# Prompt's attention between the k tiles of the gate panels, in a one-core decoder layer

## The reference

```python
h = rmsnorm(x); z = h @ w_in                       # q, k, v, u, s, m and three gates
o_da = differential attention (8 heads, T5 bias)   # prompt causal; samples over 512 paged keys + 8 new
o_sg = gelu(u) * (causal 128x128 mixing of rmsnorm(gelu(s)) + b)
o_mx = cross attention, 4 heads, 256 memory tokens # prompt: its own memory; samples: caches
gates = sigmoid(zg)
merged = g0 * (o_da @ wb0) + g1 * (o_sg @ wb1) + g2 * (o_mx @ wb2)
x = x + merged @ w_out
x = x + (silu(a) * b) @ w_down,  a, b = rmsnorm(x) @ w_up
y = rmsnorm(x)
```

## Time and profile before

| | us |
|---|---|
| median of 3 runs | 1431.42 (1426.54 to 1432.24) |
| the profiled execution, its own time | 1428.93 |
| its span, first to last instruction | 1427.2 |
| PE busy | 1322.6 (93%) |
| DVE busy | 674.5 (47%) |
| ACT busy | 553.8 (39%) |
| mean granted clock of TensorE | 0.98 |

### The profile page before, as it was taken

One profiled execution on the slowest core, in us unless ns is written; L12 is line 12 of the kernel. 1 busy time (PEld: TensorE's weight loads), 2 busy tenths in 40 slices (PEclk: granted clock), 3 DMA queues, 4 the chain that ended last, 5 costly groups with the idle time before them and its releaser, 6 DMA issues.

```text
span 1427.2 us, 26160 instructions
## 1 busy us (share of the span) xinstructions
PE 1322.6 (93%) x9982; PEld 1240.9 (87%) x9982; DVE 674.5 (47%) x1212; ACT 553.8 (39%) x1028; POOL 59.4 (4%) x106
## 2 busy tenths in 40 slices
PE   5789999999777799999998699999899999999995
PEld 4789999999545689889997369999899999999995
DVE  5452232224785122223333233337788888883333
ACT  5342321223586232323333254335555555562221
POOL 1010000000011001001000000000000000000000
PEclk9999999999999899999999999999899999999998
DMA  5355222624000977653452902222232222312221
GB/s 195 120 165 192 80 81 74 200 96 140 30 23 8 294 239 245 203 181 114 166 176 83 401 10 74 83 79 77 77 113 88 88 88 93 111 49 94 94 89 66
DMA packets 79768, 174.16 MB, mean 122 GB/s; under 512 B 5613, under 2 KB 40685, under 8 KB 78678
## 3 DMA queue, kind: packets, MB, share of 16 engines
q1 hardware_dynamic: 77942, 166.18, 34.8%
q0 software_dynamic: 1760, 7.08, 1.4%
HBM read 163.78 MB, written 11.82 MB: 123 GB/s over the span
## 4 chain that ended last, share of the span: by engine, by line
PE 55%; issue 30%; DVE 6%; ACT 3%; DMA 3%; POOL 1%; SPq 1%; DVEq 0%; POOLq 0%; ACTq 0%
PE acc L1837 46%; DMA km_pg<-mem_k 2%; DVE w_lo L1128 1%; PE ps L2074 1%; PE ps L2051 1%; ACT w_hi L666 1%; DVE logit_p L1346 1%; PE acc L2213 1%; DMA w_raw<-w_stream 1%; ACT p_junk L834 1%; ACT logit_p L818 1%; DMA b_sel<-bias_select 1%; DVE a_p L1369 1%; PE ps L1861 1%; PE ps L1954 0%
## 5 line engine op out<-in xcount | busy, mean ns | idle before, releaser
L1128 DVE TENSOR_TENSOR w_lo<-w_raw,w_hi 128x1024 fp32r<-128x1024 f32 x144 | 176.7, 1228 | 436.0 <-ACT w_hi L666 435.1
L1837 PE MATMUL acc<-h_hi,w_hi 128*128 128x288 f32 x1152 | 253.5, 302 | 1.8 <-issue 0.8
L1837 PE MATMUL acc<-h_hi,w_lo 128*128 128x288 f32 x1152 | 248.4, 297 | 0.0
L1837 PE MATMUL acc<-h_lo,w_hi 128*128 128x288 f32 x1152 | 248.4, 297 | 0.0
L666 ACT ACTIVATE w_hi<-w_raw 128x1024 fp32r<-128x1024 f32 x144 | 151.5, 1054 | 207.4 <-PE acc L1837 106.1
L1837 PEld LDWEIGHTS acc<-h_hi,w_hi 128*128 128x128 f32 x1152 | 184.6, 189 | 8.8 <-issue 6.3
L1837 PEld LDWEIGHTS acc<-h_lo,w_hi 128*128 128x128 f32 x1152 | 185.5, 189 | 0.0
L1837 PEld LDWEIGHTS acc<-h_hi,w_lo 128*128 128x128 f32 x1152 | 185.4, 189 | 0.0
L2267 PE MATMUL acc<-xs_hi,w_hi 128*128 128x288 f32 x352 | 105.7, 300 | 5.2 <-DVE w_lo L1551 4.2
L2267 PE MATMUL acc<-xs_hi,w_lo 128*128 128x288 f32 x352 | 106.0, 301 | 0.0
L2267 PE MATMUL acc<-xs_lo,w_hi 128*128 128x288 f32 x352 | 106.0, 301 | 0.0
(11 more groups left out here) (317 smaller groups left out, 2401.7 us busy)
## 6 DMA issues: line engine op xcount, KB each, us to landing
w_raw<-w_stream SPq DMA_DIRECT2D x166, 512.0 KB, 3.5
v_pg<-cache_v SPq DMA_DIRECT2D x32, 512.0 KB, 5.6
w_raw_b<-w_stream SPq DMA_DIRECT2D x22, 512.0 KB, 4.2
k_even<-cache_k SPq DMA_DIRECT2D x16, 512.0 KB, 6.1
k_odd<-cache_k SPq DMA_DIRECT2D x16, 512.0 KB, 6.2
km_pg<-mem_k SPq DMA_DIRECT2D x8, 1024.0 KB, 6.6
vm_pg<-mem_v SPq DMA_DIRECT2D x8, 1024.0 KB, 7.8
x_sb<-xT SPq DMA_DIRECT2D x8, 576.0 KB, 9.5
```

Source lines behind the costliest of these rows:

```text
L1128: nc.vector.tensor_tensor(w_lo[:, u, :], w_raw[:, u, :], w_hi[:, u, :].bitcast(F32), ALU.subtract)\
L1837: last = nc.tensor.matmul(acc[a][:, c, 0:n], w[:, u, k * P:(k + 1) * P], x[:, k0 + k, c * n:(c + 1) * n], start=start and k == 0 and t == ...
```

## The change

Eight gate panels of da_branch become a stage `da_gate` ahead of sg_branch, and prompt's attention runs inside them: after k tile k of panel c PE calls `p_step(8c + k)`. At odd steps it does turn_probs(n), values(n-1), score(n+2), n = (q-3)/2. Scores now use banks 4 and 5 alone, transposes bank 6, outputs bank 7. DVE's and ACT's order within attention is as before; ACT copies each head's output out of its bank first, and applies the gate's function after the fourth tile of a head, DVE splits the next weights after the first tile of the next head. The last steps of attention fall into the first two sg panels. Gates are stored to DRAM (`gate_d`) and loaded again for `da_proj`, eight projection panels of o_da in a row. The sigmoid becomes tanh(x/2); the 1.0 is added in the product and the 0.5 applied to `merged`. Samples begin at the half panels in S_UNIT, and SP's orders in the zone are sorted by the half panel at which they are due. The cut diff:

```diff
-STAGES = (... ("u", 8), ("sg_branch", 16), ("zm", 8), ("da_branch", 16), ("mx_branch", 16), ...)
+STAGES = (... ("u", 8), ("da_gate", 8), ("sg_branch", 16), ("zm", 8), ("da_proj", 8), ("mx_branch", 16), ...)
+S_UNIT = (2, 7, 13, 19, 24, 30, 36, 41)
 # SP
+            for c in range(KT):
+                load_w(FIRST["da_gate"] + 2 + c, c % 2)
+                if c:
+                    store_gate(c - 1)
+                if c + 2 < HEADS:
+                    sp.wait_ge(p_logit, QT * (c + 1))
+                    sp.dma_start(bias_p[c % 2], bias_pd[c + 2]).then_inc(p_bias[c % 2], 16)
+            store_gate(KT - 1)
+            for c in range(2):
+                load_w(FIRST["sg_branch"] + 2 + c, c)
+            sp.wait_ge(p_pv, TILES_P)
+            sp.wait_ge(v_zero, 1)
             value_pages(0)
+            sp.wait_ge(p_oss, HEADS)
             key_pages(1)
+            orders = [(2 * c - 1, "w", c) for c in range(2, 24)]
+            orders += [(S_UNIT[b] - 6 if b > 2 else S_UNIT[0], "k", b) for b in range(2, NB)]
+            orders += [(S_UNIT[b] - 3, "v", b) for b in range(1, NB)]
...
+            def load_gate(n):
+                if n >= 2:
+                    sp.wait_ge(acc_free[n % 2], FIRST["da_proj"] // 2 + n // 2)
+                sp.dma_start(g_slot[n % 2][:, :], gate_d[n]).then_inc(gate_loaded[n % 2], 16)
+            sp.wait_ge(gate_stored, 16 * KT)
+            sp.wait_ge(s_oout, NB)
+            load_gate(0)
+            load_gate(1)
             sp.wait_ge(o_lo_done, 2 * KT)
             for e in range(2):
+                load_w(FIRST["da_proj"] + 2 + 2 * e, 0)
+                load_gate(2 + 2 * e)
+                load_w(FIRST["da_proj"] + 3 + 2 * e, 1)
+                load_gate(3 + 2 * e)
                 mem_keys(e, e)
                 mem_values(e, e)
+            load_w(FIRST["da_proj"] + 6, 0)
+            load_gate(6)
+            load_w(FIRST["da_proj"] + 7, 1)
+            load_gate(7)
...          # kmT, vm_nat
+            stream(FIRST["da_proj"] + 8, FIRST["mx_branch"] + 2)
 # ACT, after o_split(qT, o_da[0])
-            branch("da_branch")
+            for n in range(KT):
+                p = FIRST["da_proj"] + n
+                act.wait_ge(mm_done, p + 1)
+                split_hi(p + 2, n % 2)
 # DVE
+            p_logits(0)
+            for n in range(TILES_P):
+                if n + 1 < TILES_P:
+                    p_logits(n + 1)
+                p_combine(n)
+                if n % QT == 2 and n > QT:
+                    p_norm(n // QT - 1)
+                if n % QT == 0 and n:
+                    split_lo(FIRST["da_gate"] + n // QT + 1, (n // QT - 1) % 2)
...
-            branch("da_branch")
+            for n in range(KT):
+                p, u = FIRST["da_proj"] + n, n % 2
+                split_lo(p + 2, u)
+                dve.wait_ge(mm_done, p + 1)
+                dve.wait_ge(gate_loaded[u], 16 * (n // 2) + 16)
+                wait(dve, merged_done, n)
+                nc.vector.scalar_tensor_tensor(halves(scaled[:, 0, :]), halves(g_slot[u][:, :]), 1.0, acc_t(u),
+                                               ALU.add, ALU.mult).then_inc(acc_free[u], 1)
 # PE
+            def p_step(q):
+                n = (q - 3) // 2
+                if q == 1:
+                    p_score(1)
+                if q % 2 and 0 <= n < TILES_P:
+                    p_turn_probs(n)
+                if q % 2 and 0 < n <= TILES_P:
+                    p_values(n - 1)
+                if q % 2 and 0 <= n < TILES_P - 2:
+                    p_score(n + 2)
+                if q % 8 == 0 and 0 <= q // 8 - 2 < HEADS:
+                    p_turn_out(q // 8 - 2)
+            p_score(0)
+            for c in range(KT):
+                slot_free("da_gate", c // 2, c % 2)
+                panel(FIRST["da_gate"] + c, c % 2, h_hi, h_lo, behind=lambda k: p_step(8 * c + k))
...
-            branch("da_branch", o_da, 2 * KT)
+            for n in range(KT):
+                slot_free("da_proj", n // 2, n % 2)
+                panel(FIRST["da_proj"] + n, n % 2, *o_da, tile_ready=da_tile if n == 0 else None)
```

More of the change, by code:

```diff
@@ L863, in _, with p_exps @@
-            pairs(act, p_body)
+            def p_exps(n):
+                m, e, i = n % 2, n // QT % 2, TILE_ORDER[n % QT]
+                w = (i + 1) * P
+                act.wait_ge(p_neg, n + 1)
+                wait(act, p_rc, n // QT - 1)
+                for c in range(2):
+                    last = nc.scalar.activation(logit_p[:, m, c, 0:w], logit_p[:, m, c, 0:w], ACT.Exp,
+                                                bias=col(P_NEG + 2 * m + c),
+                                                accum_out=col(P_SUM + m if c else P_S0 + 4 * e + i))
+                last.then_inc(p_exp, 1)
@@ new lines, in p_squares @@
+            def p_squares(h):
+                e = h % 2
+                act.wait_ge(p_copied, h + 1)
+                act.wait_ge(p_rc, h + 1)
+                wait(act, p_ost, 3 * (h - 1))
+                for i in range(QT):
+                    last = nc.scalar.activation(p_junk[:, i * DV:(i + 1) * DV], o_p[:, e, i * DV:(i + 1) * DV], ACT.Square,
+                                                scale=col(P_RC0 + 4 * e + i), accum_out=col(P_SS + 4 * e + i))
+                last.then_inc(p_oss, 1)
@@ L865, in s_exp_probs @@
+            p_copy(HEADS - 1)
+            p_squares(HEADS - 1)
             def s_exp_probs(b):
@@ L1395, in s_logits @@
+            split_lo(FIRST["da_gate"] + HEADS + 1, 1)
             def s_logits(b):
@@ L2038, in _, with p_score @@
-            for hp in range(HEADS // 2):
-                p_body(hp, hp == HEADS // 2 - 1)
+            def p_score(n):
+                h, i = n // QT, TILE_ORDER[n % QT]
+                w = (i + 1) * P
+                wait(pe, p_logit, n)
+                for c in range(2):
+                    rows = slice(c * DK, (c + 1) * DK)
+                    last = nc.tensor.matmul(bank(4 + c)[:, 0:w], qT[rows, h, i * P:(i + 1) * P],
+                                            kT[rows, h, 0:w], start=True, stop=True)
+                last.then_inc(p_scores, 1)
@@ new lines, in p_turn_probs, with p_values @@
+            def p_turn_probs(n):
+                m, i = n % 2, TILE_ORDER[n % QT]
+                pe.wait_ge(p_a, n + 1)
+                wait(pe, p_aT, n)
+                wait(pe, p_oout, len([h for h in range(HEADS) if 8 * h + 16 < 2 * n + 3]))
+                for j in range(i + 1):
+                    last = nc.tensor.transpose(bank(6)[:, j * P:(j + 1) * P], a_p[:, m, j * P:(j + 1) * P], ident)
+                last.then_inc(p_turn, 1)
+            def p_values(n):
+                m, h, i = n % 2, n // QT, TILE_ORDER[n % QT]
+                pe.wait_ge(p_aT, n + 1)
+                if n % QT == 0:
+                    wait(pe, p_copied, h)
+                for j in range(i + 1):
+                    last = nc.tensor.matmul(bank(7)[:, i * DV:(i + 1) * DV], aT_p[:, m, j * P:(j + 1) * P],
+                                            v_nat[:, j, h * DV:(h + 1) * DV], start=j == 0, stop=j == i)
+                last.then_inc(p_pv, 1)
```

460 lines of the change are left out of this document (186 added, 274 removed).

## The result

| | before | after |
|---|---|---|
| median of 5 runs each | 1429.07 us | 1444.05 us (1440.2 to 1446.58) |
| the profiled execution (span) | 1428.93 (1427.2) | 1446.51 (1444.8) |
| PE busy | 1322.6 | 1334.5 |
| DVE busy | 674.5 | 673.3 |
| ACT busy | 553.8 | 525.7 |

The changed kernel takes 1.0103 of the time of the kernel before, with a 95% interval of 1.008 to 1.0126. It is 15.0 us slower by the medians and 17.6 by the spans; the forecast was +9.5, so 1441. All medians are over fast runs; one slow run of e4_end (2371 us) and one of e7_pages_only (3234 us) are left out.

What follows compares the result with a forecast made beforehand. TensorE was taken as the bound or nearly so in four of five stretches. The terms -4 - 11 + 18.6 + 5.7 = +9.3, called +9.5, on 1431.4 gave 1441 us; forecast's own range 1432 to 1450, wider range 1418 to 1458.

Steps and rivals of the forecast that it cites:

- Part 1: Prompt's attention between gate panels: DVE's logits and combine alternate with PE's breaks, 16.5 us a head; -4 us (-12 to +8).
- Part 2: Stretch of the samples: the first sample gets 13.6 us shorter, less added breaks and a late panel; together -11 us.
- PE paces attention: Rival for prompt's attention: 13 us a head in place of 16.5, -28 us, 1413 us; chance 0.10.
- 1 for a late panel 5 (0 to 5): Stretch of the samples: 1 us allowed for panel 5 coming late, bounds 0 to 5.
- Part 3: da_branch as eight projection panels: +18.6 us for split and chained weight orders, and +5.7 us at the end.
- the chain: Projection: each product, gate load, weights, splits and next product follow in turn, 7.5 or 12.6 us against 6.4 a panel.
- The first wait: Start of the projection: PE waits for the split of attention's output, which nothing covers; +3.8 us.
- The handover: End of the projection: last product ends 9 us after the last matmul, 3.3 before; +5.7 us (0 to 8).
- Part 4: Gates by tanh: removed table loads on ACT stand before work whose stage is full on PE; costed at nothing.
- Weights didn't keep pace: Rival for the projection: weights keep pace, the chain's 14.8 us and most of 5.7 go; about 1421 us, chance 0.12.
- the first sample did not wait as a whole: Rival for the samples: the first still waits, pages and weights collide as before; +13, 1454 us, chance 0.10.
- The clock did fall: Rival for attention and projection: PE's idle pieces lower the granted clock, gate panels +19 us; 1460 us, chance 0.12.

Runs made afterwards that it cites:

- e4_end: Kernel after with e1_weights_ahead's early projection weights, plus the memory branch's first two weights ordered between the last gates, ahead of the memory reads: 1424.58 us.
- e7_pages_only: Kernel after with page numbers read into registers before the wait for the pages' place, order of weights unchanged: 1440.5 us.
- e2_combine_first: Kernel after with one swap on DVE in attention, combine(n) ahead of logits(n+1): 1430.06 us.
- c1_all: Kernel after with the edits of e4_end, e2_combine_first, e5_zone and e6_split_early together: 1395.2 us, ratio 0.9763 to the kernel before.
- e1_weights_ahead: Kernel after with projection weights ordered ahead of the wait for the lows and no longer behind gate loads: 1426.87 us.
- e5_zone: Kernel after with the samples' weights ordered half a panel earlier, ahead of pages, and page numbers read before the wait: 1436.92 us.
- b1_weights_before_pages: Kernel before with sg panel 2's weights ordered ahead of the first pages, v_new zeroed early, and a changed wait before sample 1's key pages: 1427.3 us.
- e6_split_early: Kernel after with the high and low parts of attention's outputs made half a panel earlier, during the last zm panel: 1438.52 us.
- c3_sigmoid: c1_all with the gates by sigmoid again in place of tanh: 1410.17 us, ratio 0.9839 to the kernel before.
- b2_combine_first: Kernel before with the edit of e2_combine_first alone, DVE's combine of a tile ahead of the next tile's logits: 1457.3 us.

## Why the prediction was right, point by point

**Direction and size.** Slower by over 0.5%, as forecast, and the median lies in the range; it is 3 us above the forecast. Some of this closeness is luck. The difference measured is +15.0 for +9.5, a miss of 5.5. The forecast was counted from a kernel before at 1431.4, whose median over five runs is 1429.07, and that took 2.3 off the miss. Part 1 came out 2.1 better and hid as much of part 2's miss.

**Part 1 held.** 16.2 us a head for 16.5, and the end at 504.4 for 506.9 (500.8 to 506.5 in the other executions). The mechanism, DVE's logits and combine in series with PE's break, is shown by e2_combine_first: with the series broken the waits are gone. What the rival "PE paces attention" said of the mechanism was wrong in one point. I had held it unlikely because one pair of banks keeps the scores from coming early. With the one pair still in place, the swap on DVE alone brings PE to its own pace. Whether a second pair would do it in the old order was not run. That pace is 14.15 us a head and not 13.

**Part 2 failed.** The term that was mis-sized is "1 for a late panel 5 (0 to 5)"; it measured 8.5 us of waits and 2.3 of slower matmuls (202.68 busy for 200.40 in c1_all), and 5.9 and 2.0 in e1_weights_ahead. The rest of the part adds up: with the late weights gone (e5_zone) the zone takes 200.6 us, where 213.5 - 11 = 202.5 was forecast with that 1 us in it. The step took the landing of weights as a thing that only PE's next panel waits for. It is ACT that waits, and in ACT's order stand steps of the sample that nothing else delays. I had also not counted SP's reads of page numbers among the orders, which cost between 1 and 5 us. The same queue in the kernel before gave the same picture in b1_weights_before_pages.

**Part 3 held, term by term,** in its times and by e1_weights_ahead: 14.0 us of the 14.8 of the chain come back when weights don't stand behind gates and splits. The choice of 5.1 us, and not 6.8, for 2 MB ahead of the weights was the nearer one: products 2 and 4 came 13.7 and 12.4 after the ones before them, 13.05 in the mean, where 5.1 gives 12.6 and 6.8 gives 14.3. The first wait was 3.71 for 3.8, and e6_split_early removes it. The handover, 9.1 for 9.0, goes back to the old wait in e4_end.

**Part 4 was costed at nothing, and that is only half right.** It was reasoned in da_branch, a stage full on PE, where the loads stood before. But the change moves ACT's gates into attention and beside the samples, where exponentials stand behind them. With the sigmoid kept the changed kernel is 4 to 7 us slower, so tanh covered a loss that the other parts would have made. In c1_all it is 11 to 15. The cost of a moved step's helpers has to be asked in the new place. The count was off too: the trace before has 31 table loads, after 4, so 27 went and not the 22 or 18 of the prediction.

**The rivals.** Weights didn't keep pace, and the first sample did not wait as a whole: sample 1 scores 22.3 us after sample 0, which had been 39.5. The clock did fall in the projection, to 0.90, but the chain set the pace there: the products came on time. In the attention stretch the rival did not come true: the clock was 0.98 there. In e1_weights_ahead, without the chain's waits, the clock was 0.97 and the panels took 53.1 us and not 51.6.

**A reading that was wrong.** The prediction opens with TensorE as the bound in four of five stretches. Its own show PE full in one of the four stages listed, and busy for 71 to 77% of the other three. No term of the sum rests on it.

**What the change itself is worth.** In the kernel before PE idled 25 us in attention, and c1_all has filled nearly all of them. Beside c1_all's 1395.2, the estimate of 1418 for the kernel before with its zone in order leaves 22 us for the change together with tanh. With the sigmoid the repaired kernel takes 1410.17 (c3_sigmoid), some 7 to 11 us below that estimate, so half or more of the 22 hangs on tanh. As it was made, the change gave them away in orders written for the old place.

## What to carry to other kernels

When a step moves, write the orders of every queue anew, and ask what stands behind a load on each engine that waits for it: the late tile and the wait that costs are often on different steps. An order of two steps on one engine has no value of its own; it is right if what lies between them covers the latency of the one that is waited for, and the same swap gave 14 us here and cost 27 there. Price an instruction that looks free in the stage it goes to, and again after the stage has been repaired.

## What the runs showed of the hardware

**The granted clock in stretches with gaps.** From 400 to 440 us, the kernel after, the kernel before and b2_combine_first, in this order:

```profile
400.00:440.00 40.00, 36.48 (x246) 29.09 (x247) 23.46 (x87) 26.00 (x78) 3.08 (x6) 1.00 0.23 81
```

```profile
400.00:440.00 40.00, 29.74 (x200) 19.85 (x196) 33.27 (x132) 32.25 (x116) 5.61 (x12) 1.00 0.07 20
```

```profile
400.00:440.00 40.00, 26.84 (x145) 16.95 (x144) 25.66 (x100) 23.06 (x83) 4.21 (x9) 0.87 0.08 20
```

PE waits for 0.7 us at a time in the first, up to 1.6 in the second, up to 1.9 in the third. The first two were granted the upper level (2.4 GHz) throughout, the third was not. In the projection of the kernel after, with waits of 3.7, 4.1 and 5.2 us, 394 matmuls are busy for 57.92 us at 0.90, and for 51.60 in c1_all at 1.00: 6.3 us that no wait shows.

**Reads of page numbers cost time on SP.** SP stands 2.4 us without an order (529.49 to 531.90 in the kernel after) where its program has a wait and four such reads. Moved ahead of a wait, the groups gave between 1 and 5 us in e7_pages_only, where the transfers and their order stayed the same.
